# Releasing the second page transfer of a step at the middle of a group of score matmuls, in a paged latent attention on one core

## The reference, cut to what matters

```python
ckv_past = cache_mla_ckv[l][page_table].reshape(bs, past, KV_LORA)     # 256 latent values to a key
kpe_past = cache_mla_kpe[l][page_table].reshape(bs, past, QK_ROPE)     # 32 rotary values to a key
s = (einsum('bqhc,bkc->bhqk', q_lat, ckv) + einsum('bqhr,bkr->bhqk', q_pe, kpe)) * ATTN_SCALE
p = softmax(s)
o = einsum('bhqk,bkc->bqhc', p, ckv)
```

## Time and profile before

| | before |
|---|---|
| median of three runs | 3964.32 us (3962.59 to 3966.49) |
| the profiled execution, its time | 3958.31 us |
| span of its instructions | 3956.6 us |
| mean granted clock of TensorE | 0.947 |
| busy: PE, DVE, ACT, POOL | 91%, 41%, 22%, 6% |
| paged attention, layer 1 and layer 2 | about 1366 to 1695 us and 3303 to 3637 us of the span |

### The profile page before, as it was taken

The page is one execution under the profiler, slowest core; times in us unless marked ns, Lnnn a source line. Parts: engine busy times, 40 slices in busy tenths (PEclk is TensorE's granted clock), DMA queues, the critical chain, the costliest instruction groups (busy, mean ns, idle before and its releaser), DMA issues. The chain is left out here.

```text
span 3956.6 us, 66158 instructions
## 1 busy us (share of the span) xinstructions
PE 3591.3 (91%) x28396; PEld 2325.3 (59%) x28396; DVE 1634.3 (41%) x3024; ACT 881.7 (22%) x1770; POOL 254.7 (6%) x277
## 2 busy tenths in 40 slices
PE   5889899999989799989879889999997997998996
PEld 3556556666556477655546556566664665776654
DVE  3021025545456577633121110444543675775522
ACT  1110012222135422220022000222221552222201
POOL 0000000000000133300000000000000002331000
PEclk7989999999989899989989899999998997999998
DMA  8210111111110266633251111111111004664433
GB/s 282 48 40 22 47 32 47 54 49 54 41 33 1 97 216 235 224 117 129 73 200 27 50 33 39 34 49 54 54 49 45 8 1 159 239 241 144 170 113 118
DMA packets 282325, 362.96 MB, mean 92 GB/s; under 512 B 57124, under 2 KB 233974, under 8 KB 265512
## 3 DMA queue, kind: packets, MB, share of 16 engines
q1 hardware_dynamic: 244320, 189.73, 16.1%
q0 software_dynamic: 25808, 155.47, 11.0%
q10 hardware_dynamic: 11896, 13.44, 0.9%
HBM read 310.23 MB, written 48.35 MB: 91 GB/s over the span
## 5 line engine op out<-in xcount | busy, mean ns | idle before, releaser
L843 PE MATMUL rwkv_gate_bank<-u,rw_gate_w 128*128 128x364 f32 (+1 forms) x2304 | 792.4, 485 | 8.1 <-PEq L171 8.1
L843 PEld LDWEIGHTS rwkv_gate_bank<-u,rw_gate_w 128*128 128x128 f32 x2304 | 416.2, 191 | 227.8 <-issue 18.5
L498 PE MATMUL mla_b<-u,mla_w 128*128 128x364 f32 (+1 forms) x960 | 297.3, 472 | 27.8 <-DMA mla_w<-in_w_in_dram 27.8
L2185 PE MATMUL dec_s_bank<-u,att_q_rows 32*64 32x256 f32 x8192 | 296.7, 387 | 28.0 <-DVE kpe L2247 19.2
L2244 DVE STREAM_TRANSPOSE u<-page_ckv 128x2048 f32<-128x2048 f32 x112 | 258.1, 2305 | 105.6 <-DMA page_ckv<-in_cache_mla_ckv_dram,page_rows 102.9
L498 PE MATMUL rwp_b<-u,rwp_w 128*128 128x364 f32 (+1 forms) x864 | 266.8, 472 | 3.6 <-DMA rwp_w<-in_w_in_dram 3.6
L498 PEld LDWEIGHTS mla_b<-u,mla_w 128*128 128x128 f32 x960 | 184.1, 192 | 139.4 <-DMA mla_w<-in_w_in_dram 28.0
L2185 PEld LDWEIGHTS dec_s_bank<-u,att_q_rows 32*64 32x64 f32 x8192 | 206.5, 134 | 101.1 <-issue 69.2
L2479 PE MATMUL out_b<-merged,out_w 128*128 128x364 f32 (+1 forms) x768 | 239.3, 475 | 12.7 <-DMA out_w<-in_w_out_dram 12.7
L2209 PE MATMUL dec_o_bank<-page_ckv,cq 128*64 128x256 f32 x1792 | 234.7, 381 | 16.0 <-DVE att_o_all L2270 14.3
L498 PE MATMUL conv_b<-u,conv_w 128*128 128x364 f32 (+1 forms) x768 | 238.5, 474 | 5.1 <-DMA conv_w<-in_w_in_dram 5.1
(11 more groups left out here) (467 smaller groups left out, 4523.8 us busy)
## 6 DMA issues: line engine op xcount, KB each, us to landing
merge_sig<-gates_feature_major SPq DMA_DIRECT2D x16, 1632.0 KB, 8.3
mod_w<-in_w_ada_dram SPq DMA_DIRECT2D x12, 2048.0 KB, 13.8
rw_gate_w<-in_w_in_dram SPq DMA_DIRECT2D x48, 512.0 KB, 4.0
gates_feature_major<-rwkv_gate_stage SPq DMA_DIRECT2D x96, 182.0 KB, 1.9
mla_w<-in_w_in_dram SPq DMA_DIRECT2D x18, 512.0 KB, 4.0
rwp_w<-in_w_in_dram SPq DMA_DIRECT2D x18, 512.0 KB, 4.0
u<-x_feature_major SPq DMA_DIRECT2D x8, 1088.0 KB, 14.2
out_x<-x_feature_major SPq DMA_DIRECT2D x16, 544.0 KB, 5.3
```

The costliest lines, as they stand in the source:

```text
L498: mm = pe.matmul(self.banks[j % len(self.banks)][:, 0:m], self.w[:, n % self.NW, k, :], s.u[:, k, t0:t0 + m], start=(k == 0), stop=(k == K ...
L843: mm = pe.matmul(self.banks[j % 2][:, 0:m], self.w[:, n % GATE_CHUNKS, k, :], self.s.u[:, k, t0:t0 + m], start=(k == 0), stop=(k == KD - 1))
L2185: mm = pe.matmul(S[64 * half:64 * half + NQ, 512 * i:512 * i + NK], q, keys, start=(cb == 0), stop=(cb == BLOCKS))
```

## The change

A new semaphore `half_scored` is raised by one by the last matmul of block `cb = 4` of each step's scores (`BLOCKS` is 8, so `BLOCKS // 2` is 4), that is by the 40th of the 72 matmuls. The odd transfer waits for that of step `k + 2` in place of the end of that step's scores. Everything else stays: the wait for `valued`, the even transfer, the order on every engine, the number of instructions on POOL.

```diff
@@ page_attention
         turned, scored, group_topped = (ph.sem(n) for n in ("turned", "scored", "group_topped"))
+        half_scored = ph.sem("half_scored")
...
                     if o >= NS:
                         pool.wait_ge(valued, 2 * ((o - NS) // 2 + 1))
                         if o % 2:
-                            pool.wait_ge(scored, 8 * ((o - NS) // 2 + 3))
+                            pool.wait_ge(half_scored, (o - NS) // 2 + 3)
                         pages.load(pool, o)
...
                                 if cb == BLOCKS:
                                     mm.then_inc(scored, 1)
+                        if cb == BLOCKS // 2:
+                            mm.then_inc(half_scored, 1)
```

## The result

| | before | changed |
|---|---|---|
| median of 6 runs each | 3965.4 us (3961.4 to 3973.97) | 3992.74 us (3990.11 to 4006.71) |
| span of the profiled execution | 3956.6 us | 3992.2 us |
| steps 2 to 29, layer 1 and layer 2 | 279.45, 279.30 us | 299.90, 293.72 us |

The ratio is 1.0075, 95% interval [1.0053, 1.0097]. The forecast was 3950.8 us, range 3942 to 3962: the sign is wrong. The kernel before was measured at about 3965 us in this comparison and in one of the later sittings (the runs e), and at 3935 to 3939 us in all the others. In the profiles taken in the 3965 us sittings the weight loads of the scores pause as in the earlier trace rows; in those taken in the others they hardly do (there it was the kernels run beside the kernel before that were profiled, not that kernel itself).

What follows compares the result with a forecast made beforehand. TensorE sets the pace, stalled by `merge` behind the odd page; at 9.72 us a step, layer 1 gains 7.3 us and layer 2 6.2, together 13.5: 3964.3 - 13.5 = 3950.8 us, range 3942 to 3962.

Steps and rivals of the forecast that it cites:

- What bounds the kernel: Attention steps 2 to 29: TensorE sets the pace and loses time before the values, waiting for `merge`, late behind the odd page.
- The increment costs nothing: Scores: the new increment rides on an existing matmul, so TensorE gets no instruction more; costed at nothing.
- The release moves by 1.8 us: Scores: signalled at the 40th of 72 matmuls, the odd page is issued at about 1447.15 in place of 1448.95.
- The same 5.96 us from issue to use: Odd page transfer: issue to use stays 5.96 us, so DVE's mean wait falls from 2.5 to 0.7 us.
- A pause that comes with an issue: Scores' weight loads: issuing a pair costs about 0.9 us; the odd pair's pause would fall in the values, costed at 0.
- Rival 1: Last 0.8 us of scores: the odd issue pauses them 0.85 us in each of 56 steps; 34 us slower, chance 0.10.

Runs made afterwards that it cites:

- the runs e: Three kernels, two from the changed one, one without the second wait, whose reduction also waits for a POOL fill after the odd pair; 1.0087, 1.0086, 1.058.
- a1: Kernel before plus the new signal in mid-scores, with the odd transfer still waiting for the scores' end; 3934.3 us, ratio 0.9994.
- c1: The changed kernel, unaltered, run again beside the kernel before in another sitting; 3913.83 us, ratio 0.9939.
- e3: Kernel before without the odd transfer's wait for scores, plus a 128x640 POOL fill (marker) after each odd pair that the reduction awaits; 4193.5 us, 1.058.
- e2: Changed kernel plus a 128x1 POOL fill (marker) after each odd pair that the reduction awaits; 3999.23 us, ratio 1.0086.

## Why the prediction was wrong, point by point

- **What bounds the kernel**: right for the old release. In the kernel before and in `a1` the odd page's arrival is what delays `merge`, and issuing it earlier lets TensorE go on sooner; without the pauses the change gains 0.6% (`c1`).
- **The increment costs nothing**: right where it was tried by itself (`a1`, 0.9994, without the pauses).
- **The release moves by 1.8 us**: right without the pauses, from 5.17 (`a1`) to 3.26 us of the step (`c1`). In the result it moved from 5.96 to between 3.26 and 4.14 us, 1.8 to 2.7 us, since most scores pause less ahead of the 40th matmul.
- **The same 5.96 us from issue to use**: right in direction, wrong in size. In `c1` it is 7.0 us. In the profile of the result DVE waits for a page only once, for 0.3 us, but only because its reduction is so late that the page is there.
- **The step that failed** is the last one, "A pause that comes with an issue", with its sentence "I cost it at 0". I took the even pair's pauses for something that only stops weight loads, saw that the odd pair's would fall into the values, and took the values' unchanged 3.60 us for cover. That was wrong in two ways. First, the scores' signal has no such cover: the last score matmul ends about 1 us after the issue, and the signal reaches DVE only 2.95 to 3.2 us after it. I priced TensorE's instructions and never asked who waits for what TensorE signals in that time. The values were not untouched either: from the first start to the last recorded end they take 4.03 us on average in place of 3.68, which costs nothing here only because the turns wait longer still for the exponential. Second, the cover was read from rows that could not show a late signal. In the kernel before, the odd issue came 0.90 us after the scores' end, when that signal was already through; the next one, of the values' end, was due 2.7 us after the issue (1448.95 to 1451.65) and was acted on at 3.04 us (the even issue at 1451.99), so it was hardly late (its two updates are at 1451.66 and 1451.74). The old wait thus kept GpSimd quiet until the scores had been reported, and the change took that away.
- **Rival 1, slower, 3998 us at a chance of 0.10**: the right sign and nearly the right time, by luck, and half the right cause (an issue inside the scores). Its mechanism, a further pause in the scores of every step, did not occur: the scores got shorter on average, 4.87 us in place of 5.09, and the values start earlier. Only in 8 of the 56 steps do the scores have a further, long pause (1.5 to 2.7 us, where the kernel before has one of 0.9 us); it begins between 0.5 us ahead of the odd issue and 0.4 us behind it, its cause is open, and since those steps take 10.97 us against 10.54 for the others it is worth about 3 us. The term is 56 steps x 1.16 us of late turns, less 30 us gained, not 56 x 0.85 less 13.
- **The condition**: the forecast took the pauses as fixed. They are not; with them the change costs 0.75%, without them it brings 0.6%.

What is shown and what is not. Shown: the late reduction is the loss; it is TensorE's signal that is late, not DVE's answer to it; it keeps a fixed distance to the odd issue over 48 steps; it does not occur in executions whose weight loads do not pause; it is not POOL's recorded work; and in the pausing condition four issues in a row cost the scores 5.4 us (`e3`). Open: whether the issue or the start of the transfer behind it holds TensorE up, since every kernel run in that condition moved both, and only the steady flow of the data is ruled out; how the late signals and the stopped weight loads hang together; and what puts an execution in that condition. It goes with a sitting, not with the kernel, and one and the same chip showed both (the second and the fourth sitting). The rule of the Trainium skill that the prediction named ("Runtime: NRT & Kernel Launch", Instruction fetch mechanics: blocks of instructions are fetched ahead, the cost mostly hidden) was put to no test by a run. But the trace of before speaks for it: its page lists a DMA queue "instruction", and 80 transfers of 16 KB of it fall in the 56 steps, at changing places. Only in 18 steps is one of them under way while the two regular pauses of the weight loads (1.08 to 2.2 us of the step) last, and the pauses are in all 56. So it is not such a transfer that these pauses wait for.

## What to carry to other kernels

When an issue is moved to overlap an engine's work, list the signals that the engine must deliver in the 3 us after it and who waits for them, and not only whether its instructions still have cover. A wait that looks too strict may be what keeps two things apart. Before it is relaxed, look in the trace for pauses put down to "issue" that keep a fixed distance to another engine's instruction, and price them at every place to which the change moves that instruction. And where a kernel of before has two levels of time between sittings (3965 and 3937 us), a change is measured at both: here the best version at one level, no second wait (0.9867 to 0.9885), is likely the worst at the other (`e3`, the same with a marker, 1.058).

## What the runs showed of the hardware that was not expected

- In the pausing condition, after an indirect transfer is issued by GpSimd, TensorE's weight loads stop from about 1.75 us on and come through in small groups about 0.7 us apart (`e3`), and TensorE's semaphore updates come up to 3.2 us after the issue, 1.9 to 2.2 us after the last recorded matmul end, where 0.05 to 0.3 us is usual (48 of 56 steps of the result, against the kernel before and `c1`). A matmul's recorded end is thus no proof that its signal is out.
- The hold ends about 1.9 us after the start of the last issue of a row, with two issues (`e2`, 1.90) as with four (`e3`, 1.93).
- Four issues in a row stretched scores of 4.1 us to 9.5 us, and the granted clock was at the 1.2 GHz level for 3.2 us behind the hold.
- Without the pauses none of this occurs with the same program, and the kernel before is 0.7% faster.
- An odd page issued 3.9 us after the even one (at -0.65 and 3.26 us of the step) took 7.0 us from issue to use; issued 5.8 us after it, 5.95 us.
